# Reordering work at the border of two stages and inside the attention unit of a two-block transformer kernel

## What is computed

```
hn   = rms_norm(h) ; proj = hn @ w_in
p_a  = rwkv7 inputs (r, k, v: 6 tiles of 128 columns; decay, a, gate low ranks: 1 tile)
p_b  = retention inputs (q, k, v, gate: 4 heads of 64)
p_c  = latent attention inputs (384 + 256 + 32 columns)
y_a  = rwkv7_mixer(p_a)              # token shift with mu; tanh(wd) @ w2, ad @ a2, sigmoid(gd) @ g2
y_b  = silu(g) * retention * rsqrt(mean(retention^2) + eps)   # the retention norm
y_c  = causal softmax attention, 8 heads, queries and keys of 64 + 32
h    = h + concat(y_a, y_b, y_c) @ w_out ; then a gated feed-forward
```

## Time and profile before

| | |
|---|---|
| median of 3 runs | 3816.51 us (3810.84 to 3816.89) |
| the profiled execution | 3816.76 us, its span 3814.9 us |
| busy: PE / DVE / ACT / POOL | 3270.0 (86%) / 1443.0 (38%) / 1111.4 (29%) / 269.3 (7%) us |
| granted TensorE clock, mean | 0.923 of full |
| DMA | 601.99 MB, mean 158 GB/s |

### The profile page before, as it was taken

One profiled execution on the slowest core, in us unless ns is written; L12 is line 12 of the kernel. 1 busy time (PEld: TensorE's weight loads), 2 busy tenths in 40 slices (PEclk: granted clock), 3 DMA queues, 4 the chain that ended last, 5 costly groups with the idle time before them and its releaser, 6 DMA issues. The chain is left out here.

```text
span 3814.9 us, 42208 instructions
## 1 busy us (share of the span) xinstructions
PE 3270.0 (86%) x16302; PEld 2316.5 (61%) x16302; DVE 1443.0 (38%) x2418; ACT 1111.4 (29%) x1899; POOL 269.3 (7%) x272
## 2 busy tenths in 40 slices
PE   4998999989588877887774978889998988969997
PEld 3776778778433333333333846768886846858886
DVE  4772466653420000000103555443323556353332
ACT  3672566652100000000002243232222244232221
POOL 0000222210000000000000001300000000400000
PEclk9999999999799999999996985989999986989999
DMA  3223222223599999999984200033323300023332
GB/s 95 61 67 64 78 56 67 67 62 116 217 417 426 426 426 425 423 422 412 418 339 136 66 12 4 1 94 95 98 96 85 83 12 4 1 78 94 97 97 77
DMA packets 355527, 601.99 MB, mean 158 GB/s; under 512 B 72288, under 2 KB 306560, under 8 KB 330624
## 3 DMA queue, kind: packets, MB, share of 16 engines
q1 hardware_dynamic: 346112, 590.85, 42.4%
q0 software_dynamic: 9216, 8.42, 0.7%
HBM read 603.40 MB, written 20.97 MB: 164 GB/s over the span
## 5 line engine op out<-in xcount | busy, mean ns | idle before, releaser
L1729 PE MATMUL ex_up<-ex_W,ex_XT 128*64 128x512 f32 x1024 | 256.9, 659 | 87.4 <-DMA ex_W<-in_w_expert_up_dram 87.4
L226 ACT ACTIVATE f_hi<-f_raw 128x1024 fp32r<-128x1024 f32 x148 | 156.8, 1059 | 565.6 <-PE ff_bk L286 550.0
L1729 PE MATMUL ex_gp<-ex_W,ex_XT 128*64 128x512 f32 x1024 | 246.4, 636 | 61.8 <-DMA ex_W<-in_w_expert_gate_dram 60.4
L235 DVE TENSOR_TENSOR f_lo<-f_raw,f_hi 128x1024 fp32r<-128x1024 f32 x148 | 181.1, 1224 | 257.4 <-ACT f_hi L226 257.2
L284 PE MATMUL ff_bk<-h_a_hi,f_hi 128*128 128x512 f32 x704 | 275.9, 392 | 2.8 <-DVE h_a_lo L3457 2.8
L285 PE MATMUL ff_bk<-h_a_lo,f_hi 128*128 128x512 f32 x704 | 275.4, 391 | 0.0
L286 PE MATMUL ff_bk<-h_a_hi,f_lo 128*128 128x512 f32 x704 | 275.3, 391 | 0.0
L1758 PE MATMUL ex_yp<-ex_W,ex_hT 128*64 128x512 f32 x1024 | 226.8, 594 | 37.0 <-DMA ex_W<-in_w_expert_down_dram 22.2
L1772 DVE TENSOR_TENSOR ex_hid<-ex_sg,ex_up 128x512 f32<-128x512 f32 x32 | 22.0, 688 | 610.7 <-PE ex_up L1729 610.7
L1729 PEld LDWEIGHTS ex_up<-ex_W,ex_XT 128*64 128x64 f32 x1024 | 93.0, 150 | 250.7 <-issue 250.7
L1729 PEld LDWEIGHTS ex_gp<-ex_W,ex_XT 128*64 128x64 f32 x1024 | 88.7, 146 | 218.6 <-issue 216.8
(11 more groups left out here) (599 smaller groups left out, 6543.9 us busy)
## 6 DMA issues: line engine op xcount, KB each, us to landing
ex_W<-in_w_expert_gate_dram SPq DMA_DIRECT2D x64, 2048.0 KB, 28.8
ex_W<-in_w_expert_up_dram SPq DMA_DIRECT2D x64, 2048.0 KB, 29.1
ex_W<-in_w_expert_down_dram SPq DMA_DIRECT2D x64, 2048.0 KB, 28.9
b_raw<-in_w_in_dram SPq DMA_DIRECT2D x88, 512.0 KB, 3.9
f_raw<-in_w_gate_up_dram SPq DMA_DIRECT2D x88, 512.0 KB, 3.9
f_raw<-in_w_down_dram SPq DMA_DIRECT2D x44, 512.0 KB, 3.5
m_raw<-in_w_in_dram SPq DMA_DIRECT2D x40, 512.0 KB, 4.0
b_raw<-in_w_branch_ssd_dram SPq DMA_DIRECT2D x16, 512.0 KB, 4.0
```

Of the source, the lines that this page charges most:

```text
L226: a.activation(self.hi[n % self.SLOTS][:, at], self.raw[n % self.RAW][:, at], ACT.Copy).then_inc(self.cast, 1)
L235: v.tensor_tensor(self.lo[i][:, at], self.raw[n % self.RAW][:, at], self.hi[i][:, at].bitcast(F32), ALU.subtract).then_inc(self.split_done, 1)
L1729: ins = pe.matmul(ps[part[e], :], XT[b][:, q, part[e]], row_view(slots[e], KD)[:, q, :], start=(q == 0), stop=(q == KD - 1))
```

## The change

It has four parts, in both layers:

1. `normalize` runs ahead of the last tile's `finish` on VectorE; its square root on ScalarE runs ahead of the last `take`. Its last multiply writes back to its own buffer, now `ret`, which outlives the stage, and no longer waits for the last matmul. GpSimd copies `ret` into `mix` at the start of stage_mix, behind its two copies of the keys and a drain.
2. The low-rank tile is the first of the seven (`RKV_ORDER`). Tanh and sigmoid are taken in stage_inputs, behind the copy of the second of the seven tiles; the semaphore `low_ready` goes.
3. In stage_mix TensorE starts with the queries of the first pair of heads, then does the low ranks; ScalarE takes these queries first.
4. In each attention unit ScalarE does take_out(u - 2) ahead of take_weights(u) and exps(u + 2).

```
+RKV_ORDER = (6, 0, 1, 2, 3, 4, 5)
-            ... + [at(n * P, P) for n in range(7)])
+            ... + [at(n * P, P) for n in RKV_ORDER])
...
@@ stage_inputs @@
-        R, y, ... = sb("R", [P, NT, 2, 64]), sb("y", [P, NT, 4, 64]), ...
+        R, y, ... = sb("R", [P, NT, 2, 64]), ret, ...
@@ scalar @@
                 for n in range(RKV, MIXED):
                     W.make_hi(a, n + 2)
+                    if n == MIXED - 1:
+                        ret_root_of()
                     take(n)
-                ret_root_of()
+                    if n == RKV + 1:
+                        a.wait_ge(out_ready, order(RKV) - KROPE + 1)
+                        a.activation(rkv[0:32, 6, :], rkv[0:32, 6, :], ACT.Tanh)
+                        a.activation(rkv[64:128, 6, :], rkv[64:128, 6, :], ACT.Sigmoid)
@@ vector, finish @@
-                        v.scalar_tensor_tensor(rkv[:, n - RKV, :], d[:], mus[:, n - RKV:n - RKV + 1], uu[:, 1:], ALU.mult, ALU.add)
+                        slot = RKV_ORDER[n - RKV]
+                        v.scalar_tensor_tensor(rkv[:, slot, :], d[:], mus[:, slot:slot + 1], uu[:, 1:], ALU.mult, ALU.add)
@@ vector, normalize @@
-                    v.wait_ge(W.used, MIXED)
-                    v.tensor_tensor(mix[:, :, RW:2 * RW], y[:]..., vg[:, :, RW:], ALU.mult)
+                    v.tensor_tensor(y[:]..., y[:]..., vg[:, :, RW:], ALU.mult)
@@ vector, end @@
                 take_y(3)
+                normalize()
                 finish(RKV + 6)
-                normalize()
@@ stage_mix, gpsimd @@
                 ins.then_inc(kr_ready, 1)
+                g.drain()
+                g.tensor_copy(mix[:, :, RW:2 * RW], ret[:].rearrange("p c h e -> p c (h e)"))
@@ tensor @@
                 def low_ranks():
-                    pe.wait_ge(low_ready, 1)
...
+                queries(0, bk[7]).then_inc(q_ready, 1)
                 low_ranks()
-                queries(0, bk[7]).then_inc(q_ready, 1)
@@ scalar @@
-                a.activation(rkv[0:32, 6, :], rkv[0:32, 6, :], ACT.Tanh)
-                a.activation(rkv[64:128, 6, :], rkv[64:128, 6, :], ACT.Sigmoid).then_inc(low_ready, 1)
+                a.wait_ge(q_ready, 1)
+                take_queries(0, bk[7]).then_inc(q_taken, 1)
                 a.wait_ge(wa_ready, 1)
...
-                a.wait_ge(q_ready, 1)
-                take_queries(0, bk[7]).then_inc(q_taken, 1)
                 a.wait_ge(q_rope_mm, 1)
...
                 for u in range(UNITS):
+                    if u >= 2:
+                        take_out(u - 2)
                     take_weights(u)
                     if u + 2 < UNITS:
                         exps(u + 2)
-                    if u >= 2:
-                        take_out(u - 2)
                     extras(u)
@@ second_layer @@
+                ret = k.sb(f"ret{l}", [P, NT, 4, 64], F32, c_out, "right")
```

More of the change, by code:

```diff
@@ L2059, in mixer_tiles, with stage_inputs @@
     return ([at(lat0 + n * P, P) for n in range(5)] + [at(krope0 - 64, 96)] + [at(RW_IN + n * P, P) for n in range(4)]
-            + [at(RW_IN + (2 + n) * RW, RW, rows) for n in range(2) for rows in halves] + [at(n * P, P) for n in range(7)])
+            + [at(RW_IN + (2 + n) * RW, RW, rows) for n in range(2) for rows in halves] + [at(n * P, P) for n in RKV_ORDER])
 @stage
-def stage_inputs(k, l, W, M, mu, q_norm, kv_norm, rkv, rqk, krT, vg, latT, cos32, sin32, mix):
+def stage_inputs(k, l, W, M, mu, q_norm, kv_norm, rkv, rqk, krT, vg, latT, cos32, sin32, ret):
     nc = k.nc
@@ L2073, in stage_inputs @@
         kd, qd, kt, inn = sb("kd", [P, 2, T]), sb("qd", [P, 2, T]), sb("kt", [P, NT - 1, RW]), [sb(f"inn{i}", [P, 4, P]) for i in range(2)]
-        R, y, yc, ss = sb("R", [P, NT, 2, 64]), sb("y", [P, NT, 4, 64]), sb("yc", [P, NT, 4, 64]), sb("ss", [P, NT, 4])
+        R, y, yc, ss = sb("R", [P, NT, 2, 64]), ret, sb("yc", [P, NT, 4, 64]), sb("ss", [P, NT, 4])
         bk = k.banks(ctx, 8, f"in{l}_bk")
@@ L2263, in finish @@
                         v.drain()
-                        v.scalar_tensor_tensor(rkv[:, n - RKV, :], d[:], mus[:, n - RKV:n - RKV + 1], uu[:, 1:], ALU.mult, ALU.add).then_inc(out_ready, 1)
+                        slot = RKV_ORDER[n - RKV]
+                        v.scalar_tensor_tensor(rkv[:, slot, :], d[:], mus[:, slot:slot + 1], uu[:, 1:], ALU.mult, ALU.add).then_inc(out_ready, 1)
                     else:
@@ L2338, in normalize @@
                     v.drain()
-                    v.wait_ge(W.used, MIXED)
-                    v.tensor_tensor(mix[:, :, RW:2 * RW], y[:].rearrange("p c h e -> p c (h e)"), vg[:, :, RW:], ALU.mult)
+                    v.tensor_tensor(y[:].rearrange("p c h e -> p c (h e)"), y[:].rearrange("p c h e -> p c (h e)"), vg[:, :, RW:], ALU.mult)
                 v.memset(u[0][:, 0:1], 0.0)
@@ L2431, in stage_mix @@
 @stage
-def stage_mix(k, layer, M, at, rkv, krT, latT, w_kv_up, cos32, sin32, v_first, out, eb, vt, gt, bonus, mix):
+def stage_mix(k, layer, M, at, rkv, krT, latT, w_kv_up, cos32, sin32, v_first, out, eb, vt, gt, bonus, ret, mix):
     nc = k.nc
@@ L2453, in stage_mix @@
         sem = lambda n: k.sem(f"mx{layer}_" + n)
-        (kv_loaded, low_ready, wa_ready, g_ready, sig_done, gt_taken, v1_ready, low_v_ready, v2_ready, vsig_ready, sq_ready, v_done, root_in, root_ready,
+        (kv_loaded, wa_ready, g_ready, sig_done, gt_taken, v1_ready, low_v_ready, v2_ready, vsig_ready, sq_ready, v_done, root_in, root_ready,
          cum_ready, exp_ready, exp_used, rk_in, kr_ready, q_ready, k_ready, q_rope_mm, qr_ready, turn_ready, q_rope, q_taken, k_taken, v_ready, v_taken) = (sem(n) for n in (
-             "kv_loaded", "low_ready", "wa_ready", "g_ready", "sig_done", "gt_taken", "v1_ready", "low_v_ready", "v2_ready", "vsig_ready", "sq_ready", "v_done", "root_in",
+             "kv_loaded", "wa_ready", "g_ready", "sig_done", "gt_taken", "v1_ready", "low_v_ready", "v2_ready", "vsig_ready", "sq_ready", "v_done", "root_in",
              "root_ready", "cum_ready", "exp_ready", "exp_used", "rk_in", "kr_ready", "q_ready", "k_ready", "q_rope_mm", "qr_ready", "turn_ready", "q_rope", "q_taken",
@@ L3264, in second_layer @@
                 M.open(k)
+                ret = k.sb(f"ret{l}", [P, NT, 4, 64], F32, c_out, "right")
                 rqk, vg = k.sb(f"rqk{l}", [P, 4, T], F32, c2), k.sb(f"vg{l}", [P, NT, 2 * RW], F32, c2)
-                stage_inputs(k, l, W, M, g("rw_mu"), g("mla_q_norm"), g("mla_kv_norm"), rkv, rqk, krT, vg, latT, cos32, sin32, mix)
+                stage_inputs(k, l, W, M, g("rw_mu"), g("mla_q_norm"), g("mla_kv_norm"), rkv, rqk, krT, vg, latT, cos32, sin32, ret)
             sb = lambda n, shape: k.sb(f"rw_{n}{l}", shape, F32, c_out, "right")
@@ L3270, in second_layer @@
             vt, gt, bonus = sb("vt", [P, NT, RW]), sb("gt", [P, NT, RW]), sb("bonus", [P, 16])
-            stage_mix(k, l, M, spent_h + 4 * KD * T, rkv, krT, latT, g("mla_w_kv_up"), cos32, sin32, v_first, out, eb, vt, gt, bonus, mix)
+            stage_mix(k, l, M, spent_h + 4 * KD * T, rkv, krT, latT, g("mla_w_kv_up"), cos32, sin32, v_first, out, eb, vt, gt, bonus, ret, mix)
         stage_delta(k, l, out, eb, vt, gt, bonus, rkv, spent_h + 4 * KD * T, g("rw_gn_w"), g("rw_gn_b"), mix)
```

## The result

The changed kernel takes 3760.47 us (median of 4 runs, 3755.85 to 3762.83) against 3813.68 us of the kernel before on the same chips; the ratio is 0.9859, 95% interval 0.9843 to 0.9875. The direction was right, the size was not. The profiled execution took 3755.85 us, span 3754.1. It is the fastest of its four, and the one profiled before (3816.76) is close to the slowest of its own, so the two traces lie 60.8 us apart, 8 us more than the medians.

A forecast was written before the change was run, and what follows sets the result against it. TensorE bound the prelude and, at half clock, the loop's end; VectorE bound mid-loop. Border 18.4, unit order 9.4 and loop clock 6 gave 33.8 us off 3816.51, so 3783; own range 3774 to 3791, full range 3766 to 3801.

The forecast's parts named there:

- the 18.4 of the sum: Stage border and prelude: less TensorE idle and a better clock save 9.2 us per layer, 18.4 for both.
- a loss of 3.3 us: Prelude: two stretches granted a clock of 0.72 lose 3.3 us per layer instead of 5.2.
- 9.4 us for both layers: Attention loop: taking outputs first in each unit removes TensorE waits and saves 9.4 us for both layers.
- my 4.7: Attention loop: per-layer gain of outputs first, 4.2 us from counted waits and 0.5 for small ones.
- case C: Border and loop: the clock holds nearly everywhere, 49 us saved, 3767 us; chance 0.15.
- The sum: Border and prelude 18.4, loop order 9.4 and loop clock 6 us: 33.8 us saved, 3783 us.
- The loop's term: Attention loop, both layers: 9.4 us from the order in the unit and 6 us from the clock.
- B: Border and loop: the clock falls as before, 24 us saved, 3793 us; chance 0.25.
- D: Attention loop: the order in the unit buys nothing and the clock is as before, 14.6 us saved, 3802; chance 0.06.
- E: Attention loop: the output's take delays the weights on ScalarE, costing 30 us less 14.6 of the border, 3832; chance 0.04.

The follow-up runs named there:

- e1: Parts 1 to 3 of the change without part 4, outputs staying behind the exponential in each attention unit: ratio 0.9947 to the kernel before.
- e8: Changed kernel plus eight unread matmuls behind the last dense tile of the input stage: ratio 0.9859 to the kernel before.
- e9: Changed kernel with part 3 undone alone, low-rank products ahead of the query products and ScalarE in the old order: ratio 0.9877 to the kernel before.
- e6: Kernel before plus two unread 128x256 matmuls in each attention unit from 21 on and one behind the loop: ratio 0.9925 to the kernel before.
- e7: Changed kernel plus two unread 128x256 matmuls in each attention unit from 21 on and one behind the loop: ratio 0.9837 to the kernel before.
- e5: Kernel before plus five unread dense 128x512 matmuls ahead of the products of the delta stage: ratio 0.9999 to the kernel before.
- e2: Kernel before with part 4 alone, outputs taken first in each attention unit: ratio 0.9912 to the kernel before.
- e11: Changed kernel plus unread matmuls behind the last dense input tile, in units from 21 on and ahead of the products: 3748.71 us, ratio 0.9823 to the kernel before.
- e3: Changed kernel with part 1 undone alone, the retention norm behind the last tile again: ratio 0.9877 to the kernel before.
- e4: The changed kernel run again unaltered for a second profile: ratio 0.9862 to the kernel before.

## Why the forecast was right or wrong

**The border (parts 1 to 3).** The mechanism and nearly the size were right. Forecast: idle of 3.1 us, gain 9.2 us per layer with a bound of 7.3 to 12.5. Measured: 3.15 us, and 10.7 and 10.5 us. e1 gives 0.9947, 20 us, for the 18.4 of the sum. The norm fitted with 0.5 us to spare, and the low-rank activations were hidden. What came on top of the forecast, 1.5 and 1.3 us per layer, is the clock: I had taken a loss of 3.3 us there, and the preludes lost 1.5 and 1.7 (20.3 and 24.2, against 18.8 and 22.5 at full clock in e8). That the queries come first had a use which I had not priced: I put part 3 at the earlier start alone, and e9 shows that the dense queries are worth 3 us per layer even with the same start, because they bring the clock back up and the low-rank products don't.

**The order in the unit (part 4).** The mechanism was right and the term was mis-sized: 9.4 us for both layers, or 15.4 with the clock, against 23.9. I counted only those waits of TensorE behind which VectorE waited in the same unit, and gave the rest to VectorE. e6 and e7 split the sum: with the clock held from unit 21 on in both orders the loops take 101.4 and 102.7 against 91.8 and 94.4, so the order alone is worth 9.6 and 8.3 us per layer, nearly twice my 4.7; the clock by itself is worth 4.3 and 6.1 in the old order, where I had taken 3, and 2.9 and 1.5 in the new one. Ahead of unit 21 the clock was not held in either, so some of what I put down to the order there may be clock as well. Still, most of the waits that I wrote off as covered were not: what came back in layer 0, 9.6 us, is close to its 12.6 us of waits. The forecast that the clock would hold at the loop's end was wrong in the trace (it fell at 2311, 15 us before the loop's end; in the kernel before it fell 30 us before it); case C's picture of a clock that never falls was too.

**What was missing.** The sum ended at the loop. It took the delta stage for untouched, since no line of it changed, although the clock was one of its terms and does not stop at a stage. The products run at 0.50 in the kernel before, but for the last 4 us in layer 1; they are 15.3 us shorter in the changed kernel's trace. This is the step that failed: "the change touches only ... two of the stages", with nothing in the sum for the stage behind them, and with it a largest gain (case C, 3767) that stopped short of 3760. The loop's term was too small as well, but with border and loop as measured (45.1 us) and nothing for the products the sum would have given 3771, inside the range. With the 15.3 us of the products in it, the sum of the measured stretches is the whole difference between the two traces.

e5 shows by itself that the clock makes the products long or short: the same instructions took 32.0, 30.2, 24.6 and 20.1 us, by the clock alone. How far the change causes this is less clear. In the kernels without added matmuls the products were short (23.2 to 23.8) in nine of ten layers with the new order in the unit (the tenth, in e9, had 32.0), and near that, 24.2, in one of six with the old; but e7 and e8, both with the new order and added matmuls, had 31.7, 27.4 and 32.0. By the medians, the change gains 53 us, of which border and loop account for 45 in the traces, so that by this estimate the products bring some 8 in a usual execution and 15 in the profiled one, which is also the fastest of its four. So short products were seen more often with the new order; that it causes them is not shown. What sets how early the clock rises behind the loop stays open; it was not tried.

**The rivals.** B (clock as before) had the border wrong by 3 us per layer. The section of the Trainium skill that spoke for it ("TensorE: Matmul & The Clock Gate", "A second HAM failure mode: psum-queue depth-cycling"), on short idle times that make the clock swing, is borne out by the loop, where the clock fell twice in layer 0 of the changed kernel although no gap there was longer than 2.6 us; it did not mean a slower kernel. C (the clock holds) came nearest by its number, which is luck: the clock fell behind the border and in the loop of both layers, and the missing gain came from the products. D (the order in the unit buys nothing) is out by e2, where that edit alone gives 0.9912. E, the take in the way of the weights, is out too: that edit alone made the kernel faster (e2), and TensorE's waits for the weights sum to 4.0 us in layer 0.

## What to carry to other kernels

When a change alters how long TensorE idles, follow its granted clock past the edited lines until a stretch where both kernels show the same value; a stage of small matmuls that no edit touched held a quarter of the difference between the two traces here (15.3 of 60.8 us). Put dense work first behind a gap. Where another engine is the bound at full clock and TensorE at half, a few unread matmuls in TensorE's waits can pay: 12 us here on top of the change (e11), and 27 without it (e6). Ahead of the products alone (e5) and at the border alone (e8) they showed no gain.

## What the runs showed of the hardware that was not expected

- Two unread matmuls in each of the last eleven units of the loop, and one behind it, made a kernel faster: e6, 0.9925.
- In the kernel before the clock stayed at half through all 32.0 us of the products of layer 0, while TensorE was busy 7.5 us of 8 with them (windows above). In e3 it stood at 0.51 for the first 5 us of the dense query products and at 1.00 behind them.
- A gap of 3.15 us was followed by half clock in layer 0 in one profile (prelude 20.3 us) and not in another of the same kernel (18.8 us). Of the ten layers with this gap (changed kernel, e1, e4, e7, e9) it was the only one without. A TensorE idle of 1.3 us did not let it fall at the border in e8 and e11, but behind the loop, after an idle of 0.97 us, it fell in both layers of e7 and in layer 0 of e11, and not in layer 1 of e11.
- VectorE's multiply of 128x1024 (`mx_t<-mx_kk`) took 1.90 us while GpSimd's copy of 128x1024 ran beside its first 0.8 us, against 1.22 in the kernel before, where it started behind GpSimd's copies. Its scaling of 128x512 took 1.24 us beside a copy of GpSimd, against 0.48 elsewhere.
